# Expert outputs accumulated into one row per token by the scatter DMA, instead of two rows per token summed at the end

## The reference, cut to what matters

```python
h = jax.nn.silu(jnp.einsum('td,edf->tef', xf, w_gate)) * jnp.einsum('td,edf->tef', xf, w_up)
y = jnp.einsum('tef,te,efd->td', h, gate.astype(h.dtype), w_down)
...
x = layer_norm(ALPHA * x + ffn, ln2_g[l], ln2_b[l])
```

## Time and profile before

| | us |
|---|---|
| median of the three runs | 1589.46 |
| the profiled execution, its own time | 1589.06 |
| its span, first to last instruction | 1587.2 |
| VectorE's last pass ends | 1582.95 |

### The profile page before, as it was taken

One profiled execution on the slowest core, in us unless ns is written; L12 is line 12 of the kernel. 1 busy time (PEld: TensorE's weight loads), 2 busy tenths in 40 slices (PEclk: granted clock), 3 DMA queues, 4 the chain that ended last, 5 costly groups with the idle time before them and its releaser, 6 DMA issues.

```text
span 1587.2 us, 24282 instructions
## 1 busy us (share of the span) xinstructions
PE 1458.6 (92%) x9497; PEld 1312.7 (83%) x9497; DVE 1012.3 (64%) x1176; ACT 760.6 (48%) x869; POOL 167.4 (11%) x95
## 2 busy tenths in 40 slices
PE   7999999999999999999996489999999999999930
PEld 6998898899999999999996378888888888888720
DVE  4234425437777787312025568888888888888828
ACT  4224333334334423311112067778887777788712
POOL 0000000000000000323330101111112111111200
PEclk9999999999999999989997599999999999999965
DMA  8221322122213312522313579999999999999965
GB/s 281 83 82 54 107 84 80 52 96 80 82 54 109 107 55 69 192 69 94 131 43 144 208 255 350 393 392 385 378 373 386 386 402 393 397 386 380 353 220 219
DMA packets 87452, 333.50 MB, mean 210 GB/s; under 512 B 12199, under 2 KB 17839, under 8 KB 57923
## 3 DMA queue, kind: packets, MB, share of 16 engines
q1 hardware_dynamic: 82340, 315.40, 53.9%
q0 software_dynamic: 5040, 17.06, 2.8%
HBM read 320.96 MB, written 31.10 MB: 222 GB/s over the span
## 4 chain that ended last, share of the span: by engine, by line
PE 84%; DVE 10%; DMA 3%; issue 1%; ACT 1%; SPq 0%; POOL 0%; DVEq 0%; POOLq 0%; ACTq 0%
PE BANK L1483 12%; PE BANK L1484 12%; PE BANK L1485 12%; PE BANK L1811 8%; PE BANK L1813 8%; PE BANK L1812 8%; PE BANK L1832 4%; PE BANK L1834 4%; PE BANK L1833 4%; PE BANK L1794 2%; PE BANK L1535 2%; PE BANK L1558 2%; PE BANK L1614 1%; DVE LO L986 1%; PE BANK L1707 1%
## 5 line engine op out<-in xcount | busy, mean ns | idle before, releaser
L1483 PE MATMUL BANK<-XH,HI 128*128 128x260 f32 x1786 | 519.5, 291 | 12.6 <-DVE XL L983 8.9
L1378 DVE TENSOR_TENSOR LOB<-RAWB,HIB 128x2048 fp32r<-128x2048 f32 x204 | 466.9, 2293 | 83.1 <-ACT HIB L884 80.1
L1484 PE MATMUL BANK<-XL,HI 128*128 128x260 f32 x1786 | 509.1, 285 | 0.0
L1485 PE MATMUL BANK<-XH,LO 128*128 128x260 f32 x1786 | 508.4, 285 | 0.0
L884 ACT ACTIVATE HIB<-RAWB 128x2048 fp32r<-128x2048 f32 x204 | 391.3, 1920 | 95.1 <-PE BANK L1813 86.2
L1483 PEld LDWEIGHTS BANK<-XH,HI 128*128 128x128 f32 x1786 | 341.3, 191 | 29.3 <-issue 28.5
L1485 PEld LDWEIGHTS BANK<-XH,LO 128*128 128x128 f32 x1786 | 341.4, 191 | 0.0
L1484 PEld LDWEIGHTS BANK<-XL,HI 128*128 128x128 f32 x1786 | 341.4, 191 | 0.0
L1811 PE MATMUL BANK<-HIB,XGH 128*128 128x512 f32 x544 | 214.5, 394 | 5.7 <-DVE LOB L1378 4.3
L1813 PE MATMUL BANK<-LOB,XGH 128*128 128x512 f32 x544 | 213.0, 391 | 0.0
L1812 PE MATMUL BANK<-HIB,XGL 128*128 128x512 f32 x544 | 212.6, 391 | 0.0
(11 more groups left out here) (305 smaller groups left out, 1490.6 us busy)
## 6 DMA issues: line engine op xcount, KB each, us to landing
RAWB<-in_w_gate SPq DMA_DIRECT2D x68, 1024.0 KB, 9.4
RAWB<-in_w_up SPq DMA_DIRECT2D x68, 1024.0 KB, 8.9
RAWB<-in_w_down SPq DMA_DIRECT2D x68, 1024.0 KB, 11.2
RAW<-in_w_in SPq DMA_DIRECT2D x39, 1024.0 KB, 5.0
RAW<-in_w_out SPq DMA_DIRECT2D x16, 1024.0 KB, 4.9
Y<-in_xT SPq DMA_DIRECT2D x8, 520.0 KB, 9.2
RT<-in_xT SPq DMA_DIRECT2D x16, 260.0 KB, 5.1
x_rows<-R SPq DMA_DIRECT2D x5, 832.0 KB
```

The costliest lines, as they stand in the source:

```text
L1378: dve.tensor_tensor(LOB[:, s, :], RAWB[:, r, :], HIB[:, s, :].bitcast(F32), ALU.subtract).then_inc(b_lo[s], 1)
L1483: pe.matmul(bank, hw[:, c, :], h, start=(c == 0), stop=False)
L1484: pe.matmul(bank, hw[:, c, :], l, start=False, stop=False)
L1485: ins = pe.matmul(bank, lw[:, c, :], h, start=False, stop=(c == KC - 1))
```

## The change

- y_rows has 520 rows, one per token. SP writes x1 (R) into it, five DMAs of 104 rows, after loads 6 and 7 of block 0; they count on a new semaphore s_y0.
- YIX uses column 0 of the table, the token, and the scatter adds to the row in DRAM (`compute_op=ALU.add`) rather than write it. A block holds a token once, and the wait on b_yw keeps two scatters apart.
- POOL waits for the five writes after gather 1 and before it clears ROWS.
- The loads of x1_rows into X2 and X8 go, and with them f_x, YA8 and YB8. After the last scatter SP loads X2 from y_rows, one DMA per tile, with X8 behind the first.
- VectorE's `added` and the samples' two sums go. ScalarE makes the mean of each tile with a Copy that is scaled by -1/D and accumulated into MV2, in front of its square; it writes YB, which the square then overwrites.

```diff
-    y_rows = nc.dram_tensor("y_rows", [2 * T, D], F32, kind="Internal").ap()
+    y_rows = nc.dram_tensor("y_rows", [T, D], F32, kind="Internal").ap()
...
             for i in range(NRAW, 8):
                 bload(i, None, (a["w_gate"], a["w_up"])[i % 2][0, :, 2048 * (i // 2):2048 * (i // 2) + 2048], 0)
+            for i in range(NT):
+                sp.dma_start(y_rows[i * TT:(i + 1) * TT, :], R[:, i, :]).then_inc(s_y0, 16)
...
-            sp.wait_ge(s_x1w, 16 * NT)
-            for i in range(NF):
-                sp.dma_start(X2[:, i, :], x1_rows[128 * i:128 * i + 128, :]).then_inc(f_x, 16)
-            sp.dma_start(X8[:, :, :], x1_rows[SEQ:T, :].rearrange("(g r) (c n) -> (r c) g n", g=2, c=32)).then_inc(f_x, 16)
-
...
-            sp.dma_start(YA8[:, :, :], y_rows[0 * T + SEQ:0 * T + T, :].rearrange("(g r) (c n) -> (r c) g n", g=2, c=32)).then_inc(f_in8, 16)
-            sp.dma_start(YB8[:, :, :], y_rows[1 * T + SEQ:1 * T + T, :].rearrange("(g r) (c n) -> (r c) g n", g=2, c=32)).then_inc(f_in8, 16)
             for i in range(NF):
-                for c, dst in ((0, YA), (1, YB)):
-                    sp.dma_start(dst[:, i, :], y_rows[c * T + 128 * i:c * T + 128 * i + 128, :]).then_inc(f_in[i], 16)
+                sp.dma_start(X2[:, i, :], y_rows[128 * i:128 * i + 128, :]).then_inc(f_in[i], 16)
+                if i == 0:
+                    sp.dma_start(X8[:, :, :], y_rows[SEQ:T, :].rearrange("(g r) (c n) -> (r c) g n", g=2, c=32)).then_inc(f_in8, 16)
...
-                    bounds_check=last_row, oob_is_err=False).then_inc(b_yw, 16)
+                    bounds_check=last_token, oob_is_err=False, compute_op=ALU.add).then_inc(b_yw, 16)
...
             gather(1, b_xg)
+            pool.wait_ge(s_y0, 16 * NT)
             pool.memset(ROWS[:, :], 0.0).then_inc(s_ones, 1)
...
+                act.wait_ge(f_in[i], 16)
+                act.activation(YB[:, i, :], X2[:, i, :], ACT.Copy, scale=-1.0 / D, accum_out=MV2[:, i, 0:1]).then_inc(f_mu, 1)
                 act.wait_ge(f_mu, i + 1)
...
-            ts(YIX[:, :], tab[:, 2, :], SKIP, None, ALU.add)
+            ts(YIX[:, :], tab[:, 0, :], SKIP, None, ALU.add)
...
-                dve.wait_ge(f_in8, 32)
-                done(tt(X8[:, :, :], X8[:, :, :], YA8[:, :, :], ALU.add))
-                done(tt(X8[:, :, :], X8[:, :, :], YB8[:, :, :], ALU.add))
+                dve.wait_ge(f_in8, 16)
...
-            def added(i):
-                dve.wait_ge(f_in[i], 32)
-                done(tt(X2[:, i, :], X2[:, i, :], YA[:, i, :], ALU.add))
-                done(dve.scalar_tensor_tensor(X2[:, i, :], X2[:, i, :], 1.0, YB[:, i, :], ALU.mult, ALU.add, accum_out=MV2[:, i, 3:4]))
-                ts(MV2[:, i, 0:1], MV2[:, i, 3:4], -1.0 / D, None, ALU.mult).then_inc(f_mu, 1)
-
-            dve.wait_ge(f_x, 16 * NF + 16)
             samples_sum()
             samples_centre()
-            added(0)
...
             for i in range(NF):
-                if i + 1 < NF:
-                    added(i + 1)
                 finished(i)
```

More of the change, by code:

```diff
@@ L199, in build @@
     O_8 = O_PR + NF * D * 4
-    X8, YA8, YB8, Q8 = (sb(n, [128, 2, 64], F32, O_8 + 512 * k) for k, n in enumerate(("X8", "YA8", "YB8", "Q8")))
+    X8, Q8 = (sb(n, [128, 2, 64], F32, O_8 + 512 * k) for k, n in enumerate(("X8", "Q8")))
     LG8, LB8 = (sb(n, [128, 64], F32, O_8 + 2048 + 256 * k) for k, n in enumerate(("LG8", "LB8")))
@@ L343, in build @@
         s_passed = sem("waits_passed")
-        f_x = sem("x1_in")
+        s_y0 = sem("y_rows_set")
         f_in = [sem(f"y_in{i}") for i in range(NF)]
@@ L634, in _ @@
             pool.wait_ge(s_ones, 2)
-            last_token, last_row = pool.to_reg(T - 1), pool.to_reg(2 * T - 1)
+            last_token = pool.to_reg(T - 1)
             def gather(j, landed):
```

## The result

The changed kernel takes 1600.65 us in the median of six runs (1597.99 to 1604.23), against 1589.99 for the kernel before on the same chip (1587.2 to 1594.96). The ratio is 1.0058 with an interval of 1.0044 to 1.0072: slower by 0.6%, where 0.6% faster was forecast. The profiled execution took 1598.42 us, with a span of 1596.6.

What follows compares the result with a forecast made beforehand. PE was taken to bound the expert blocks, only just, and VectorE the tail. 1589.1 - 15.1 - 3.4 + 7.6 + 2.0 = 1580.2, so 1580 us; own range 1575 to 1588, range with rivals 1569 to 1614.

Steps and rivals of the forecast that it cites:

- The tail: After the last matmul, bound by VectorE: dropping sums gains 15.1 us, halving loads gains 3.4 us.
- the sums: Tail: VectorE loses eight passes, ScalarE takes over the mean; 39.0 us become 23.9, a gain of 15.1 us.
- the loads: Tail: half the loads go, so the first tile lands sooner after the last scatter; gain 3.4 us.
- The price of a row: Scatter: an accumulating row costs a plain one plus one gather of the same bytes, taken as a doubling.
- Rival 3: Scatters in the block stage: destination read not overlapped, a row costs three plain rows; 1612 us, chance 0.23.
- point of decision: Block scatters: slower once the extra exceeds 18.5 us, put at about 2.2 times a plain row with nothing hidden.
- The last two scatters: End of the chain: the last scatter costs 2.0 us more (0 to 14), the one before it nothing.
- Setting y_rows: Five DMAs of 832 KB around block 0 fit in idle DMA room: cost nothing, or 10 us if uncovered.
- the blocks: Expert blocks: the accumulating scatter's extra bytes, less slack, cost 7.6 us (0 to 20), in nine tight blocks.
- 4.7 MB, as half, at 425 GB/s: Nine tight blocks: half of POOL's 9.4 MB counted as scatter, 11.1 us of extra DMA time before slack.
- The slack: Tight blocks: 3.5 us of the extra absorbed, since PE didn't wait with a landing of 12.8 us.
- Rival 2: Blocks: extra bytes fall on the engines already last, all scatter bytes count, 20 us; 1593 us, chance 0.21.

Runs made afterwards that it cites:

- e1: The changed kernel with a plain scatter, without the add (x1 and one of a token's two experts left out): 1570.06 us.
- e7: The kernel before with every plain scatter made twice, the second into a tensor of its own, slots not spread: 1631.73 us.
- e2: The changed kernel with y_rows set from weight data during the projections and the five writes of R removed: 1601.77 us.
- e4: The kernel before with the five writes of R added, into a tensor of their own, and POOL waiting for them: 1590.39 us.
- e3: The changed kernel with a block's slots spread over sixteen groups of partitions by permuting one constant, computation complete: 1571.17 us.
- e6: The changed kernel with slots going round sixteen groups of eight neighbouring partitions, the first 64 on only four of each: 1590.43 us.
- e5: The kernel before with its slots spread over sixteen groups of partitions by permuting one constant: 1586.26 us.
- e8: The kernel before with every plain scatter made twice and the slots spread over the partitions: 1590.56 us.

## Why the prediction was wrong

**The tail was right.** 15.1 us were forecast for the sums and 15.6 came; 3.4 for the loads and 3.7 came. ScalarE and VectorE alternate every 4.7 us, as forecast.

**The price of a row was right.** The forecast took the doubling. The queue's share times 16 engines times the span is 2.8% and 711 us before, 4.2% and 1073 us after (the shares are rounded, so either may be off by 13). The difference is 362 us; about half of the queue's 17.06 MB is scatter, some 1040 rows of 8 KB, so 0.35 us for a row on top. A plain row takes 711 / 2080 = 0.34, skipped slots included (by the records of the last scatter it is 0.31 plain and 0.63 with the add). With spread slots the same working gives 0.31 (4.3% of 1565.3 less 3.0% of 1566.7, 325 us). The Trainium skill (Collectives: The Full Stack, Stop 4, SDMA + CCE: where bytes move and the add happens) says that an add in the DMA engine is two reads and one write. The doubled time fits that, but the profile does not show the second read: packets, megabytes and the 312.44 MB that it gives as read from HBM are the same in e1 and in the changed kernel. Rival 3, at three times, falls: a row with the add takes twice a plain one, and e7 shows that two plain rows do the same harm. Its point of decision was also worked out wrong: 18.5 us over the 20 us of all scatter bytes is a row at 1.9 times a plain one with nothing hidden, and not 2.2, so the doubling that the forecast took would be past it if none of it were hidden.

**The last two scatters were right.** 12.02 us against 9.91, so 2.1 where 2.0 was forecast, and ScalarE's wait for the last but one went from 6.1 to 5.7.

**Setting y_rows was right:** nothing, by e2 and by e4.

**The step that failed is the blocks.** "4.7 MB, as half, at 425 GB/s" spread the extra over sixteen engines, let only nine of fifteen blocks pay, and took 3.5 us off for slack. 7.6 us were forecast and 26.5 came, which is over the upper end of 20 as well. "Half" was too low to begin with: in those nine blocks the scatters write 744 rows, 6.1 of the 9.4 MB, which by the forecast's own way is 14.3 us and not 11.1. And the extra is not spread over sixteen engines. It falls on those that serve the filled partitions, as e3, e6 and the rows under way in the last scatter show. By the Trainium skill's map the fullest engine has 8 rows as soon as 36 slots are filled, which they are in nine blocks (1 to 4 and 9 to 13), and it pays 8 x 0.35 = 2.8 us more in each: 25.2 us. The periods of these nine grew by 26.1 in all, the other six by 1.5, with at most 4 rows to an engine.

That match is one of totals, found after the fact, and it is no rule for a block. The nine periods grew by 0.9 to 6.0 us each, and 3.4 us of the sum are the two falls of the clock. In e3 the fullest engine still has 53 rows over the nine blocks in place of 72, which at 0.35 us is 18.6 us, and 1.1 came. Scatters 11 and 12, of 120 and 128 rows, put 8 rows on the fullest engine in any order of the slots, and yet these two periods lose 5.0 us packed and 1.1 spread. So what a block loses hangs on the blocks around it as well: on what is left over from the scatters before, and perhaps on the gather, whose rows lie on the same partitions. No run separates these. What is shown is that the extra is dear while it is packed on part of the engines and nearly free when it is spread.

**Rival 2 was the right mechanism.** It said that the extra bytes fall on the engines that are already last, gave 1593 and had a chance of 0.21. Its own size, 20 us for the blocks where 26.5 came, was short: it took all scatter bytes, but still divided them by sixteen engines. What spoke against it (landings of 9.4 us in the middle stretch) was a stretch with few rows in a block, where indeed hardly anything was lost. The argument said that no row decides it, but the trace of before held two readings that bear on it: the sixteen updates of each load, in one of them from 6.3 to 11.9 us behind its issue (7.8 to 9.8 once the slots are spread, in e5), and the rows of the last scatter, mostly 8 under way at once.

**The slack was misread.** That PE waited for nothing at a landing of 12.8 us gave 3.5 us of room. The first block with a large scatter behind it was longer already (36.3 us), and the load above lands at 16.4 us in place of 11.9. No row of before showed 3.5 us of room; it was taken from the spread between two stretches, and 12.8 us may as well have been the last value before PE waits.

## What to carry to other kernels

A DMA whose filled slots lie side by side loads only some of the engines: lay the filled slots so that every engine has its share before asking whether there is bandwidth left. A mean DMA share of 1.00 says nothing on that; look at the sixteen updates of one load, and where the last comes much later than the first, the spread is room to be had, for work that can use it (the kernel before, where PE is the bound, gained 4.5 us by it). And an accumulating row takes the engine time of two plain ones (0.63 us against 0.31 for 8 KB here), on the engine that carries it: price it there, and not on the mean of all. How much of it shows in the time depends on what else these engines have to carry, for which no formula came out of these runs. Where the waits that follow are long, look at TensorE's clock too: two falls cost 3.4 us here on top of the waits.

## What the runs showed that was not expected

- The mean DMA share was 1.00 or 1.01 in every version, with 363 GB/s (e2) to 396 GB/s (e8) in the same window. The 383 GB/s of the kernel before was no ceiling.
- An accumulating scatter holds POOL for 1.60 us at its issue where the plain one holds it for 1.02 (e1 and before), here without effect.
- One edit of a constant, with no instruction added, took 29.5 us off the changed kernel and 4.5 off the kernel before. The gather's rows are moved by the same permutation; a kernel in which only the scatter's rows are spread was not tried, so how much the gather adds is open. That packed gathers alone cost no block anything is shown by e1.
